# A retention, attention, conv and expert block: router product turned, next rows loaded later, weight ring in seven halves

## The reference

```python
def moe_swiglu(x, w_router, w_gate, w_up, w_down):
    logits = (x @ w_router).astype(jnp.float32)
    top_val, top_idx = lax.top_k(logits, TOP_K)
    wts = jax.nn.softmax(top_val, axis=-1)
    gates = jnp.sum(jax.nn.one_hot(top_idx, N_EXPERTS, dtype=jnp.float32) * wts[..., None], axis=-2)
    out = jnp.zeros_like(x)
    for e in range(N_EXPERTS):
        h = jax.nn.silu(x @ w_gate[e]) * (x @ w_up[e])
        out = out + gates[..., e:e + 1].astype(x.dtype) * (h @ w_down[e])
    return out
```

## Time and profile before

| | before |
|---|---|
| median of 3 runs | 1849.55 us (1848.19 to 1853.12) |
| the profiled execution | 1849.77 us |
| its span | 1847.6 us |
| mean granted clock of TensorE | 0.973 of full speed |
| PE busy | 1737.4 us, 94% |
| DVE busy | 1410.6 us, 76% |
| ACT busy | 1034.0 us, 56% |
| moved by DMA | 531.20 MB, mean 288 GB/s |

### The profile page before, as it was taken

How to read it: one execution, slowest core, us unless ns; L and a number is a source line. 1 busy time by engine, 2 the same in 40 slices (tenths; PEclk the granted TensorE clock), 3 DMA queues, 4 the chain that set the end, 5 groups by cost and what they waited for, 6 DMA issues and landing times.

```text
span 1847.6 us, 23317 instructions
## 1 busy us (share of the span) xinstructions
PE 1737.4 (94%) x9360; PEld 1480.0 (80%) x9360; DVE 1410.6 (76%) x1238; ACT 1034.0 (56%) x837; POOL 48.5 (3%) x44
## 2 busy tenths in 40 slices
PE   2999989998889998997999999999999999999996
PEld 2987778878579997996888887888878878888785
DVE  7796666675965555675888978979979889798897
ACT  2343434553233343334777777767777677676773
POOL 0000012000000000001000000000000000000010
PEclk8999999999989999997999999999999999999998
DMA  9687345624727563563999999999999999999994
GB/s 366 219 336 295 115 155 181 229 78 150 225 107 277 185 253 137 205 219 143 365 362 386 385 377 362 364 370 361 374 383 367 358 387 376 380 386 370 375 377 161
DMA packets 217772, 531.20 MB, mean 288 GB/s; under 512 B 7601, under 2 KB 14017, under 8 KB 217409
## 3 DMA queue, kind: packets, MB, share of 16 engines
q1 hardware_dynamic: 210624, 514.52, 76.2%
q10 hardware_dynamic: 5712, 10.41, 1.5%
q0 software_dynamic: 1328, 4.73, 0.7%
HBM read 521.94 MB, written 16.09 MB: 291 GB/s over the span
## 4 chain that ended last, share of the span: by engine, by line
PE 67%; DVE 5%; DMA 3%; ACT 2%; issue 2%; POOL 0%; SPq 0%; DVEq 0%; POOLq 0%; ACTq 0%
PE psum L792 21%; PE psum L794 21%; PE psum L793 21%; DVE units L1662 2%; DMA ring<-in_moe_w_gate 2%; PE psum L1167 1%; DMA ring<-in_moe_w_up 1%; ACT units L1539 1%; PE psum L1068 1%; DVE R L2013 0%; PE psum L1021 0%; PE psum L1105 0%; PE psum L1140 0%; PE psum L1132 0%; POOL root_out L1611 0%
## 5 line engine op out<-in xcount | busy, mean ns | idle before, releaser
L1662 DVE TENSOR_TENSOR units<-ring,units 128x2048 fp32r<-128x2048 f32 x451 | 1011.3, 2279 | 248.7 <-ACT units L1292 144.5
L1539 ACT CAST units<-ring 128x2048 fp32r<-128x2048 f32 x332 | 625.2, 1913 | 239.8 <-PE psum L794 82.0
L792 PE MATMUL psum<-units,xr 128*128 128x512 f32 x1120 | 445.1, 397 | 14.8 <-DVE units L1662 7.3
L794 PE MATMUL psum<-units,xr 128*128 128x512 f32 x1120 | 439.9, 393 | 0.0
L793 PE MATMUL psum<-units,xr 128*128 128x512 f32 x1120 | 439.2, 392 | 0.0
L1292 ACT CAST units<-ring 128x2048 fp32r<-128x2048 f32 (+1 forms) x119 | 218.6, 1882 | 214.9 <-PE psum L794 188.4
L792 PE MATMUL psum<-units,H 128*128 128x512 f32 x696 | 273.4, 393 | 4.4 <-DVE H L1662 4.4
L794 PE MATMUL psum<-units,H 128*128 128x512 f32 x696 | 271.5, 390 | 0.0
L793 PE MATMUL psum<-units,H 128*128 128x512 f32 x696 | 271.4, 390 | 0.0
L792 PEld LDWEIGHTS psum<-units,xr 128*128 128x128 f32 x1120 | 212.4, 190 | 62.6 <-DVE units L1662 7.4
L792 PE MATMUL psum<-xr,units 128*128 128x256 f32 x864 | 248.7, 288 | 7.3 <-DVE xr L1662 3.8
(11 more groups left out here) (263 smaller groups left out, 996.9 us busy)
## 6 DMA issues: line engine op xcount, KB each, us to landing
ring<-in_moe_w_gate SPq DMA_DIRECT2D x56, 2048.0 KB, 9.7
ring<-in_moe_w_up SPq DMA_DIRECT2D x56, 2048.0 KB, 9.9
ring<-in_moe_w_down SPq DMA_DIRECT2D x56, 2048.0 KB, 9.7
ring<-in_mod_w SPq DMA_DIRECT2D x12, 2048.0 KB, 9.8
ring<-in_ret_w_in SPq DMA_DIRECT2D x11, 2048.0 KB, 9.5
ring<-in_fox_w_in SPq DMA_DIRECT2D x8, 2048.0 KB, 7.9
ring<-in_sc_w_in SPq DMA_DIRECT2D x6, 2048.0 KB, 8.1
ring<-in_ffn_w_gate SPq DMA_DIRECT2D x5, 2048.0 KB, 9.4
```

Of the source, the lines that this page charges most:

```text
L792: mm(dst, left[0], right[0], start=first, stop=False)
L794: return mm(dst, left[1], right[0], start=False, stop=last)
L1539: nc.scalar.copy(*expert_unit_parts(q, j, half, 0)).then_inc(unit_high, 1)
L1662: return v.tensor_tensor(dst, src, high.bitcast(F32), ALU.subtract)
```

## The change

Four things are changed.

- The router product has the router's columns as weights and the tokens moving, pair by pair as ScalarE hands them over. The result, 8 x 256, is copied to SBUF and turned back by two transposes.
- In the routing, the order on VectorE is another: the two memsets come earlier; the split of chunk 1 is done by halves, one between choice and rank and one behind the selection; the weights of the two experts, the sums' start and the overflow test come behind the gather. The gather is handed over in two halves.
- The rows of the next expert are asked for in front of chunk 8, not 4.

```diff
+ROWS_BEFORE = 8
...
+HALVES = 2 * RING + 1
...
-        ring = sb("ring", [P, RING, ROWS * D])
+        ring = sb("ring", [P, HALVES, ROWS * D // 2])
...
+        scoresT = R[0:NE, 10752:10752 + T]
...
+        def expert_slot(h):
+
+            s = h % HALVES
+            return 2 * RING if s == 0 else (2 * LOADED + s - 1) % (2 * RING)
...
                 sp.wait_ge(rows_placed, 2 * NT * 16)
-                sp.wait_ge(gate_emptied, 2)
-                sp.wait_ge(up_emptied, 2)
+                sp.wait_ge(sums_begun, NT)
                 sp.wait_ge(gather_filled, e)
...
                 for j in range(PER_EXPERT):
-                    if j == 4 and more:
+                    if j == ROWS_BEFORE and more:
                         load_rows_of(e + 1, 1 - q)
-                    sp.wait_ge(unit_ready, e * (2 * PER_EXPERT) + 2 * (PRE + j - RING) + 2)
...
+                    for half in range(2):
+                        h = 2 * j + half
+                        sp.wait_ge(unit_ready, e * (2 * PER_EXPERT) + 2 * PRE + h + 1 - HALVES)
...
+                        sp.dma_start(dst, src.rearrange("o p k n -> (o p) k n")).then_inc(half_filled[expert_slot(h)], 16)
...
             transpose_scaled("x5T", z_mix1, 2)
-            wait_emptied("x5T", 3)
+            b = take_bank("routeT", 0)
+            for k in range(KB):
+                if k % 2 == 0:
+                    wait_emptied("x5T", k // 2)
+                last = mm(b[0:NE, 0:T], w_router[:, k, :], x5T[:, k, :], start=(k == 0), stop=(k == KB - 1))
+            last.then_inc(bank_filled, 1)
+            wait_emptied("routeT", 0)
             b = take_bank("route", 0)
             for tt in range(NT):
-                for k in range(KB):
-                    last = mm(b[:, tt * NE:(tt + 1) * NE], x5T[:, k, tt * P:(tt + 1) * P], w_router[:, k, :],
-                              start=(k == 0), stop=(k == KB - 1))
+                last = nc.tensor.transpose(b[:, tt * NE:(tt + 1) * NE], scoresT[:, tt * P:(tt + 1) * P], ident[0:NE, 0:NE])
...
+                    if k == KB // 2 - 1:
+                        last.then_inc(first_gathered, 1)
...
-                if j == 0:
+                if first:
+                    pe.wait_ge(first_low, 1)
+                elif j == 0:
                     pe.wait_ge(gather_emptied, e + 1)
...
-                s = (LOADED + j) % RING
-                act.wait_ge(slot_filled[s], e * (16 * PER_EXPERT // RING) + 16 * ((LOADED + j) // RING + 1))
                 for half in range(2):
+                    h = 2 * j + half
+                    act.wait_ge(half_filled[expert_slot(h)], e * (16 * 2 * PER_EXPERT // HALVES) + 16 * (h // HALVES + 1))
...
+            act.wait_ge(first_gathered, 1)
+            nc.scalar.copy(e_x[0][0][:, 0:4, :], psum[:, 0, :].rearrange("p (k t) -> p k t", k=4)).then_inc(first_high, 1)
+            act.wait_ge(gather_filled, 1)
+            nc.scalar.copy(e_x[0][0][:, 4:8, :], psum[:, 1, :].rearrange("p (k t) -> p k t", k=4)).then_inc(gather_high, 1)
...
             select(0, 0)
+            low_half(CHUNK_AT["sc_out", 1] + 2, 1)
+            dve.wait_ge(first_high, 1)
...
+            gates()
             places()
-            gathered(0, 0)
+            for q in range(NT):
+                first_sums(q)
+            dve.wait_ge(up_emptied, 2)
+            overflow()
+            dve.wait_ge(sums_begun, NT)
...
-    nc = bacc.Bacc("TRN2", target_bir_lowering=False, num_devices=1)
+    nc = bacc.Bacc("TRN2", target_bir_lowering=False, num_devices=1, dynamic_dma_scratch_size=8192)
```

More of the change, by code:

```diff
@@ L250, in bank_plan @@
     g += [("x5T", i, "A") for i in range(4)]
-    g += [("route", 0, "D"), ("rank", 0, "D")]
+    g += [("routeT", 0, "D"), ("route", 0, "D"), ("rank", 0, "D")]
     return g
@@ L468, in build @@
         returned = sem("returned")
+        half_filled = [sem(f"half_filled{s}") for s in range(HALVES)]
         slot_filled = [sem(f"slot_filled{s}") for s in range(RING)]
@@ L590, in pre_load @@
                 width = chunk_width(n)
-                return as_cols(ring[:, s], KB)[:, :, 0:width], cols(w, at + COLS * i, width)
+                return as_cols(slot, KB)[:, :, 0:width], cols(w, at + COLS * i, width)
             blocks = chunk_blocks(n)
-            return as_rows(ring[:, s], ROWS)[:, 0:blocks, :], rows(ROW_SOURCES[name], ROWS * i, blocks)
+            return as_rows(slot, ROWS)[:, 0:blocks, :], rows(ROW_SOURCES[name], ROWS * i, blocks)
         def unit_parts(n, half):
             size = ROWS * D // 2
-            src = ring[:, loaded_at(n) % RING, half * size:(half + 1) * size]
+            if n < PRE:
+                src = ring_slot(loaded_at(n))[:, half * size:(half + 1) * size]
+            else:
+                src = ring[:, expert_slot(2 * (n - PRE) + half), :]
             dst = [units[:, (2 * n + half) % UNITS, i, :] for i in range(2)]
@@ L1149, in wide_product @@
                 for half in range(2):
+                    if first and half == 1:
+                        pe.wait_ge(gather_emptied, 1)
                     w = expert_unit(e, q, j, half, lambda a: as_cols(a, 4))
@@ L1241, in _ @@
             gather(0, 0)
-            wide_product(0, 0, 0)
+            wide_product(0, 0, 0, first=True)
             sweeps(pe, expert, start_second)
@@ L1664, in _, with low_half @@
             split = [0]
+            def low_half(m, half):
+                dve.wait_ge(unit_high, 2 * m + half + 1)
+                src, dst = unit_parts(m, half)
+                low(dst[1], src, dst[0]).then_inc(unit_ready, 1)
             def lows_until(n):
@@ L2164, in _ @@
             normed("mix1", 3, from_banks("sc_y"), z_mix1)
+            step(v.memset(rt[:, :, :, :], 0.0))
+            step(v.memset(slot_of[:, :, :], -1.0))
             shift_rows(3, z_mix1)
@@ L2172, in wide @@
                 return rt[:, i, :, 0:1].to_broadcast([P, NT, NE])
-            lows_until(CHUNK_AT["sc_out", 1] + 2)
-            step(v.memset(rt[:, :, :, :], 0.0))
+            v.tensor_copy(scoresT, bank("routeT", 0)[0:NE, 0:T]).then_inc(emptied["D"], 1)
             v.tensor_copy(rt[:, LG].rearrange("p t e -> p (t e)"), bank("route", 0)[:, 0:NT * NE]
@@ L2206, in _ @@
-            for q in range(2):
-                step(v.tensor_reduce(big[:, q:q + 1], b[0:1, 2 * NE:3 * NE], AX.X, ALU.max))
-                ins = v.tensor_scalar(over[:, :], big[:, q:q + 1], float(P), None, ALU.is_gt)
-                ins.then_inc(turn_emptied, 1)
-            dve.wait_ge(turn_emptied, 2)
-            v.tensor_copy(big[:, 0:1], b[0:1, 0:1]).then_inc(emptied["D"], 1)
+            v.tensor_copy(counts[:, :], b[0:1, 2 * NE:3 * NE]).then_inc(emptied["D"], 1)
             dve.wait_ge(emptied["D"], ALL_EMPTIED["D"])
@@ L2213, in _, with gates @@
             dve.wait_ge(scatter_emptied, 1)
-            dve.wait_ge(up_emptied, 2)
-            dve.wait_ge(gate_emptied, 2)
+            v.memset(big[:, 0:1], 0.0).then_inc(gate_emptied, 2)
+            v.memset(big[:, 1:2], 0.0).then_inc(up_emptied, 2)
+            def gates():
+                dve.wait_ge(lg_exp, 1)
+                step(v.tensor_scalar(rt[:, 13, :, 0], rt[:, EX, :, 0], 1.0, None, ALU.add))
+                step(v.reciprocal(rt[:, G1, :, 0], rt[:, 13, :, 0]))
+                step(v.tensor_tensor(rt[:, G2, :, 0], rt[:, G1, :, 0], rt[:, EX, :, 0], ALU.mult))
+                step(v.tensor_tensor(rt[:, LG], rt[:, OH1], wide(G1), ALU.mult))
+                step(v.tensor_tensor(rt[:, LG2], rt[:, OH2], wide(G2), ALU.mult))
+                step(v.tensor_tensor(gate_of[:, :, :].rearrange("p e t -> p t e"), rt[:, LG], rt[:, LG2], ALU.add))
@@ L2218, in places, with first_sums, overflow @@
+            def first_sums(q):
+                v.tensor_scalar(e_acc[:, q, :], x[:, q, :], ALPHA, None, ALU.mult).then_inc(sums_begun, 1)
+            def overflow():
+                for q in range(2):
+                    step(v.tensor_reduce(big[:, q:q + 1], counts[:, :], AX.X, ALU.max))
+                    v.tensor_scalar(over[:, :], big[:, q:q + 1], float(P), None, ALU.is_gt).then_inc(turn_emptied, 1)
+                dve.wait_ge(turn_emptied, 2)
             def places():
```

65 lines of the change are left out of this document (34 added, 31 removed).

## The result

The changed kernel took **1829.24 us** (median of 4 runs, 1828.87 to 1833.49) beside 1851.17 for the kernel before: ratio 0.9888, 95% interval 0.9867 to 0.991, so 17 to 25 us faster. The forecast was 1835.6 and its range ended at 1831: the sign was right, the gain was put a third too low.

The account below looks back on a forecast made before the run. TensorE was taken as the bound, with the weights only just keeping up. Gains of 6.2 us at the start and 8.0 from the ring, 14.2 in all, off 1849.77 gave 1835.6 us, range 1831 to 1845.

Parts of the forecast that it names:

- The ring: Experts 3, 5 and 7: seven 1 MB halves freed one by one end the late loads; gain 8.0 us (4 to 8.2).
- The rival that the ring was not the cause: Experts 3, 5, 7: ScalarE's stop and VectorE's additions stall TensorE with any ring; 1843.6, or 1839.6 us; 14%.
- Loads of 1 MB: Rival at every expert load: 1 MB loads cost bandwidth and the kernel gets slower, about 1890 us; 6%.
- The router: Router product with tokens moving: idle time and half clock product saved, less new copy and transposes; gain about 1.0 us (-0.3 to 2.5).
- Choice to gather: Routing: scalings, overflow test and a memset leave VectorE's way to the gather; gain 1.8 us (1.5 to 2.1).
- Gather to first product: Gather handed over in halves, first half converted while the second runs; gain 2.3 us, 3.9 with the clock's 1.6.
- Expert 0: First products at full clock gain 1.6 us; VectorE's work moved behind the gather delays chunk 2, -0.5 us (0 to -2.5).
- the third rival: Routing and expert 0: VectorE's backlog and the extra router step eat the early gain; 1841.8 us; 6%.
- The start in all: Routing through expert 0's first chunks: all gains there less VectorE's backlog; 6.2 us (2 to 8).
- The loop's jumps: Experts 2 and 4, where the loop over expert pairs jumps back: 9.4 us of loss, untouched by the change.
- The rows: Next expert's rows asked for before chunk 8, not 4: SyncE doesn't stand still in expert 0; 0 us in later experts.
- The scratch: Smaller scratch frees 8 KB per partition for the seventh half; can only touch GpSimd's eight indirect transfers; 0 us.

Follow-up runs that it names:

- the ring in the kernel before: Kernel before with seven 1 MB halves in place of three 2 MB slots, small scratch, next rows before chunk 8, old routing: 1840.19 us, ratio 0.994.
- the first run: Changed kernel with three 2 MB slots, old scratch and next rows before chunk 4, so only the new routing is left: 1851.97 us, ratio 1.0006.
- the rows in front of chunk 4 again: Changed kernel, seven halves kept, with the next expert's rows asked for before chunk 4 instead of 8: 1839.36 us, ratio 0.9933.

## Why the prediction was right in sign and wrong in size

**The ring, +8.0: right**, in size and place. Experts 3, 5 and 7 gave back 1.5 + 1.9 + 4.6 us. Some luck is in the size: in the five profiles with whole slots this loss was 3.5 to 10.6 us, and the kernel before, with 8.0, stood near their mean of 7.2; in the thirteen with halves it was never over 0.2. What I named as the reason was only half of it: I counted on a round of seven halves, and six halves do as well. A load of 1 MB lands in 8.5 us in the median, not in the about 7 I took, so the slack was nearer 6.6 us than 8. The rival that the ring was not the cause fell with the ring in the kernel before, which won 11 us.

**Loads of 1 MB: the rival fell.** Clean stretches move 380 to 385 GB/s with halves of 1 MB and 384 with 0.5 MB, as with 2 MB in the earlier trace rows, and in a full queue halves land 2.71 us apart, below the 2.8 that I had set as the sign of this rival. Of the two readings of the Trainium skill that I had weighed (DMA: Bandwidth & Descriptors), the rate of a single 1 MB transfer under Bandwidth, Measured doesn't carry over to a full queue, and the one under Anatomy of one DMA, a fixed cost mostly in the receipt, from which I had concluded that it is hidden, agrees with these rows. Both are given there for transfers that GpSimd issues; the loads here are SyncE's.

**The router, +1.0: mis-sized; it gave 3.7.** The failing step is "256 columns cost 0.38, at the low clock perhaps 0.43: 16 records, 6.0 to 6.9 us". They took 4.56, since the granted clock rose at 844.1 in the middle of them and eleven of the sixteen records took 0.22. The 0.38 was twice the mean of a gather that itself ran at both clocks (0.21 and 0.11 a record), so it was the cost at neither. The turned product follows the transposes without the old 1.8 us of idle time, at 256 columns a matmul. I had named this case and given it 1.5 us in the bound of this term, instead of reading what half of the product at full clock saves. The new steps (copy, transposes, handoffs) took 0.9 us rather than 1.5: 0.42 for the copy, 0.30 for both transposes, which are two records, not four, and ran at full clock too.

**Choice to gather, +1.8: 2.3. Gather to first product, +2.3 before the clock: 2.9. Expert 0, +1.6 for the clock and -0.5 for VectorE's backlog: +0.5.** The 1.6 was too high: expert 0 of before was only 1.33 us longer than 79.96 (six matmuls at 0.43, not eight). The backlog was real: after the 48 matmuls of chunks 0 and 1, chunk 2's first half comes late behind the gates and places, and TensorE stands 0.70 us. So the sign that I had set for the third rival, VectorE named before the third chunk, came, and the rival didn't: it was set without a size.

```profile
868.50 2.30 DVE units L1699
870.80 0.04 issue
870.85 0.50 PE psum L814
```

The start in all gave 9.5 us against 6.2 (bounds 2 to 8). Taken from the same early part, TensorE's first expert product stands at 854.6, where I had said 858.

**The loop's jumps, "I keep those 9.4 us": wrong by 3.4.** Written-out experts show that the stall belongs to the jump, as I said, but its length is not fixed. In five profiles with the old ring the two stretches took 84.25 us on average (ten stretches), in nine with halves and the loop 82.7 (eighteen). I had also misread the row: at 1107.41 VectorE began to split the half, and it was ready at 1109.71. Of the 3.2 us that TensorE stood, 2.0 were a wait for this half and 1.22 were without a named cause. The rows behind those of the earlier trace rows:

```profile
1109.71 1.22 issue
1110.92 0.49 PE psum L792
```

In expert 2 of after the jump reads:

```profile
1098.42 1.92 ACT units L1573
1100.42 1.77 issue
1102.33 0.24 issue
1102.58 2.29 DVE units L1699
1104.87 0.25 issue
1105.12 0.49 PE psum L814
1105.61 0.23 PE psum L815
```

Beside the earlier trace rows the steps of ScalarE and VectorE are the same and stand at the same distance from the start of the stretch (1.2 and 5.3 us). What is shorter is TensorE's own step behind the ready half, 0.25 us instead of 1.22, and its matmuls go on at 0.23 instead of 0.43: the loss was 2.4 us, against 3.4 (4.99 less eight matmuls at 0.20 more), and the clock stayed up. In expert 4 TensorE waited 1.82 at 1342.57, all of it without a named cause, and the clock fell anyway, another 1.6 us (eight matmuls of 0.43). The ring in the kernel before shows that the gain comes with the halves; how they shorten TensorE's step at the jump stays open.

**The rows, 0: right as a term, and wrong as a thought.** By itself the move is worth nothing (1850.20), without it the changed kernel loses 8 us. I had written that SyncE thus doesn't stand still in expert 0, and given it no price, so I did not see that the start's gain hung on it. It did the sum no harm since the change has both. The same holds for "the start gives nothing": that rival would have been right without the rows, by a mechanism (SyncE's order) that I had not named.

**The sum**: 14.2 + 3.3 (start) + 3.4 (jumps) + 0.1 = 21.0, to rounding the 20.9 that the profiles show at the same early part. So two steps failed: the router's product, priced at the low clock, and the stalls at the jumps, kept whole. **The range** failed at its low end: it added the whole bounds of start and ring and nothing for a stall that I had declared out of reach, and the start came out above its bound of 8.

The scratch was not tried alone; it is in the ring's kernel and in the changed one. Its 0 has no sign against it in the chains shown here, but it is not measured. GpSimd's scatter is on the chain where SyncE stands at the rows: with the old scratch its last landing took 4.24 us (the first run), with the smaller one 4.25 (the rows in front of chunk 4 again).

## What to carry to other kernels

A gain on one engine counts only if the queue that feeds it next is not standing at something that the same change made later: here the routing's 9 us were worth 0 or 9, by where one small load stood in SyncE's order. Free and refill a ring in the pieces in which it is consumed before making it deeper: here six halves did what seven did. Compare spans from a common point behind the parts that are alike, since one and the same part of 834 us varied here by 5 us from profile to profile.

## What the runs showed of the hardware that was not expected

TensorE's clock rose from 1.2 to 2.4 GHz within the router's product, when TensorE had been busy without a pause from 840.39 to 844.1 with transposes and float32 matmuls of 256 columns; before, where 1.84 us of idle time stood between the transposes and 32 records of 8 columns, it stayed at 0.50 for all 7.0 us. With matmuls in the idle places it never fell in the routing.

A jump back of a loop stopped TensorE 1.3 to 3.5 us (28 jumps in fourteen profiles), and the same code written out not at all, although that is new code too. In the trace of after, packets of 16 KB of the instruction queue stand some 25 us apart all through the experts, and at the jump before expert 2 there are two more (1102.4 and 1107.5 us). That the engines wait for these is likely and not shown.

Loads of 2, 1 and 0.5 MB in a full queue moved data at one rate, 387 GB/s (5.42, 2.71 and 2.71 us for 2 MB, 1 MB and a pair of 0.5 MB), with 21, 42 and 84 of them per expert.
